# Two transformer blocks on one core: layer 0 as two streams with attention dealt among projections, expert weights in contiguous rows

## What is computed

```python
# first block, layer 0 (both streams) and layer 1 (x only, the context gives keys and values)
mx, mc = silu(c) @ ada_w[l] + ada_b[l], silu(c_ctx) @ ada_w[l] + ada_b[l]    # shift, scale, gate, twice
hx, hc = modulate(rmsnorm(x), mx), modulate(rmsnorm(ctx), mc)
yx, yc = mixer(hx, hc)      # layer 0: x attends to x (windowed or full) and to ctx; ctx attends to ctx only
x   = x   + gate_x * rmsnorm(yx);  x   = x   + gate_x2 * rmsnorm(swiglu(modulate(rmsnorm(x))))
ctx = ctx + gate_c * rmsnorm(yc);  ctx = ctx + gate_c2 * rmsnorm(swiglu(modulate(rmsnorm(ctx))))   # layer 0 only
# second block: h @ w_in, a gated recurrence (HGRN), a spatial gating unit, out projection, then
aff = softmax(h @ router_w);  gate, idx = top_k(aff.T, 32)                 # 16 experts choose 32 tokens each
hid = silu(xs @ w_gate) * (xs @ w_up)                                      # (32, 2048) per expert
x   = x + g_f * scatter_add((hid @ w_down) * gate)
```

## Time and profile before

| | us |
|---|---|
| median of 3 runs | 2781.61 (2778.0 to 2782.05) |
| the profiled execution | 2776.35 |
| its span | 2774.4 |
| PE busy in the span | 2235.6 (81%) |
| DVE, ACT busy | 576.9, 408.5 |
| HBM read | 610.49 MB, 220 GB/s over the span |

### The profile page before, as it was taken

The page is one execution under the profiler, slowest core; times in us unless marked ns, Lnnn a source line. Parts: engine busy times, 40 slices in busy tenths (PEclk is TensorE's granted clock), DMA queues, the critical chain, the costliest instruction groups (busy, mean ns, idle before and its releaser), DMA issues.

```text
span 2774.4 us, 25106 instructions
## 1 busy us (share of the span) xinstructions
PE 2235.6 (81%) x10537; PEld 1154.7 (42%) x10537; DVE 576.9 (21%) x1238; ACT 408.5 (15%) x814; POOL 6.2 (0%) x13
## 2 busy tenths in 40 slices
PE   6999988999999899899987789775555555565555
PEld 3444443444444446688834677641111111111111
DVE  3126823000000437200031582310000000000001
ACT  2014533000000325300032122110000000000000
POOL 0000000000000000000000000000000000000000
PEclk9999999999999999999999898987788778778876
DMA  9538841121222210243611231389999999999997
GB/s 367 219 160 307 314 138 61 61 81 42 63 78 68 91 61 31 92 151 103 201 61 61 70 112 70 129 342 418 417 416 417 418 418 418 418 416 416 417 418 300
DMA packets 198800, 613.17 MB, mean 221 GB/s; under 512 B 5360, under 2 KB 98800, under 8 KB 156448
## 3 DMA queue, kind: packets, MB, share of 16 engines
q1 hardware_dynamic: 197824, 608.28, 56.9%
q0 software_dynamic: 864, 3.28, 0.4%
HBM read 610.49 MB, written 1.05 MB: 220 GB/s over the span
## 4 chain that ended last, share of the span: by engine, by line
PE 48%; DMA 31%; DVE 5%; ACT 1%; issue 1%; DVEq 0%; ACTq 0%
PE ps L330 47%; DMA ring<-in_expert_w_up 12%; DMA ring<-in_expert_w_down 12%; DMA ring<-in_expert_w_gate 7%; PE ps L669 1%; DVE AR L635 1%; DVE X L636 1%; DVE AR L1254 0%; DVE AR L1242 0%; DVE AR L1243 0%; ACT H L581 0%; DVE AR L1135 0%; DVE AR L1231 0%; DVE AR L1232 0%; ACT RS L557 0%
## 5 line engine op out<-in xcount | busy, mean ns | idle before, releaser
L330 PE MATMUL ps<-ring,AR 128*32 128x512 f32 (+1 forms) x4096 | 523.2, 659 | 373.9 <-DMA ring<-in_expert_w_up 139.5
L330 PE MATMUL ps<-H,ring 128*128 128x512 f32 (+1 forms) x2416 | 800.5, 493 | 21.1 <-ACT H L581 13.1
L330 PEld LDWEIGHTS ps<-H,ring 128*128 128x128 f32 x2416 | 460.9, 192 | 353.2 <-issue 305.2
L330 PEld LDWEIGHTS ps<-ring,AR 128*32 128x32 f32 x4096 | 144.6, 134 | 735.8 <-issue 257.9
L330 PE MATMUL ps<-AR,ring 128*128 128x256 f32 (+1 forms) x1024 | 299.6, 456 | 3.0 <-DVE AR L793 1.5
L330 PEld LDWEIGHTS ps<-AR,ring 128*128 128x128 f32 x1024 | 196.1, 192 | 106.2 <-issue 84.4
L330 PE MATMUL ps<-AR 128*64 128x128 f32 (+5 forms) x1168 | 213.8, 340 | 29.6 <-DVE AR L1243 9.5
L330 PEld LDWEIGHTS ps<-AR 128*128 128x128 f32 (+2 forms) x1168 | 151.0, 186 | 108.9 <-issue 81.2
L1653 DVE TENSOR_TENSOR AR<-AR,ps 128x512 f32<-128x512 f32 x16 | 11.0, 688 | 590.9 <-PE ps L330 590.9
L793 DVE TENSOR_TENSOR AR<-AR,ps 128x512 f32<-128x512 f32 (+1 forms) x44 | 24.4, 555 | 424.7 <-PE ps L330 424.7
L1639 ACT ACTIVATE AR<-ps 128x512 f32<-128x512 f32 x16 | 9.6, 597 | 548.8 <-PE ps L330 548.8
(11 more groups left out here) (220 smaller groups left out, 1100.3 us busy)
## 6 DMA issues: line engine op xcount, KB each, us to landing
ring<-in_expert_w_gate SPq DMA_DIRECT2D x64, 2048.0 KB, 24.0
ring<-in_expert_w_up SPq DMA_DIRECT2D x64, 2048.0 KB, 23.4
ring<-in_expert_w_down SPq DMA_DIRECT2D x64, 2048.0 KB, 23.9
ring<-in_ada_w SPq DMA_DIRECT2D x36, 2048.0 KB, 8.6
ring<-in_ffn_w SPq DMA_DIRECT2D x44, 1024.0 KB, 7.1
ring<-in_ffn_w SPq DMA_DIRECT2D x16, 1408.0 KB, 7.1
ring<-in_w_in SPq DMA_DIRECT2D x11, 2048.0 KB, 7.9
ring<-in_ab_w_in SPq DMA_DIRECT2D x4, 2048.0 KB, 15.9
```

The costliest lines, as they stand in the source:

```text
L330: m = nc.tensor.matmul(out_, lhsT=lhsT, rhs=rhs, start=start, stop=stop)
```

## The change

1. **Two streams in layer 0.** x and the context become streams of 256 columns with their own semaphores. `Pre` and `Post` work on one half. The context is loaded first. The projections follow `AB_ORDER`: (stream, block) with 1 the context; two condition jobs stand between.
2. **Attention by stream.** 24 context units, then 24 x units, in each the differential ones first. The work beside a unit stands between its scores and its output product. Beside the context's units: x's last projection chunks (`AB_BESIDE`) and six condition jobs of layer 0 (`ADA_BESIDE`). Beside x's units: the twelve condition jobs of layer 1 in even units and the context's output projection in odd ones. Each stream's sub-norm goes beside its windowed units. For differential units scores are issued one unit less ahead.
3. **FFN0** runs the context three weight jobs ahead of x; norms of one stream go beside the blocks of the other. The context's latent projection follows x's last block.
4. **Layer 2's condition jobs** go beside layer 1's attention. The second context is loaded and normed beside FFN1's `w2` blocks.
5. **Norm sums**: DVE folds eight squares and PE sums one tile, where PE summed eight.
6. **Expert rows**: `runs` lays weights out as `(p k) n -> p k n`, one run of 16 KB per partition. The tokens and the hidden rows are read with strides 2 and 4 to match.
7. FFN gate and up products of two chunks share a bank.

The diff, cut to its core:

```diff
+HALF = (slice(0, TX), slice(TX, T2))
+LAG = 3
...
+        def runs(w, r0, r1):
+            k, n = (r1 - r0) // P, w.shape[-1]
+            return (lambda s: ring[:, s, 0:k * n].rearrange("p (k n) -> p k n", k=k),
+                    w[r0:r1, :].rearrange("(p k) n -> p k n", p=P))
...
-        ada_jobs(1)
-        ada_jobs(2)
-        for i in range(2):
-            job(("ab_out", i), rows(A["ab_w_out"][0], 0, D, i * 512, (i + 1) * 512))
+        ab_in_job(0)
+        ab_in_job(1)
+        ada_jobs(0, range(4, 6))
+        for i in range(2, 5):
+            ab_in_job(i)
+        ada_jobs(0, range(6, 12))
+        ada_jobs(1, range(4))
+        ab_out_jobs("ab_out_ctx", (0,))
+        ada_jobs(1, range(4, 8))
+        ab_out_jobs("ab_out_ctx", (1,))
+        ada_jobs(1, range(8, 12))
+        ab_out_jobs("ab_out", range(2))
         ffn_jobs(0)
...
         job("wkv_b", rows(A["mla_wkv_b"][0], 0, KVL, 0, 2048))
+        ada_jobs(2)
...
-                job(("gu", e, i), rows(w, (i % 4) * 256, (i % 4 + 1) * 256, 0, EF))
+                job(("gu", e, i), runs(w, (i % 4) * 256, (i % 4 + 1) * 256))
-                job(("dn", e, i), rows(A["expert_w_down_2"][0, e], i * 512, (i + 1) * 512, 0, D))
+                job(("dn", e, i), runs(A["expert_w_down_2"][0, e], i * 512, (i + 1) * 512))
...
         class Pre:
             def pe(self, pe):
+                pe.wait_ge(folded[self.half].sem, self.fold + KD - 1)
+                mm(ps[:, b, 0:TX], ones, self.ACC, True, True, b)
+            def dve_fold(self, c, k):
+                c.eng.wait_ge(squares_ready[self.half].sem, self.sq + k + 1)
+                first = H[:, 0, self.t] if k == 1 else self.ACC
+                c.mark(V.tensor_tensor(self.ACC, first, H[:, k, self.t], ALU.add), folded[self.half], self.fold + k)
...
+        def dve_norms(c, post, pre):
+            for k in range(KD):
+                post.dve_add(c, k)
+                if k >= 2:
+                    pre.dve_fold(c, k - 1)
+            pre.dve_fold(c, KD - 1)
+            pre.dve_scale(c)
...
         class Attention:
             def pe(self, pe):
                 for i, u in enumerate(self.units):
+                    while given < min(n, i + 4 - len(u.maps)):
+                        self.pe_scores(pe, given)
+                        given += 1
                     b = take(pe, ("t", u.key))
...
-                    if i + 3 < n:
-                        self.pe_scores(pe, i + 3)
+                    while given < min(n, i + 5 - len(u.maps)):
+                        self.pe_scores(pe, given)
+                        given += 1
+                    self.pe_beside(pe, i)
                     b = take(pe, ("o", u.key))
...
-                    if self.pe_beside:
-                        self.pe_beside(pe, i)
...
+        FFN0 = []
+        for i in range(NW + KD + LAG):
+            if i >= LAG:
+                FFN0.append((0, i - LAG))
+            if i < NW + KD:
+                FFN0.append((1, i))
...
+        AB_ORDER = [(1, 0), (1, 1), (1, 2), (0, 0), (1, 3), (0, 1), 4, 5, (1, 4), (0, 2)]
+        AB_BESIDE = {0: 10, 2: 11, 4: 12, 6: 13, 8: 14, 10: 15}
+        ADA_BESIDE = {13: 6, 14: 7, 16: 8, 17: 9, 18: 10, 19: 11}
...
+        def dve_item(c, s, n):
+            if s == 0:
+                for cq in turning(n):
+                    dve_rope(c, rope_base + ROPED.index(cq), QK[:, cq, 0:TX], ("rot", cq), TMP, ft("cos_ab"), ft("sin_ab"))
...
+        def pe_beside_x(pe, i):
+            pe_ada_beside(pe, 1, i)
+            if i % 2 and i < 16:
+                pe_out_chunk(pe, "yc", "ab_out_ctx", i // 2, lambda k: H[:, k, TX:T2])
+            pe_subln_beside(pe, 0, i)
+        def dve_beside_x(c, i):
+            dve_ada_beside(c, 1, i)
+            if i % 2 and i < 16:
+                post0a[1].dve_chunk(c, i // 2)
+            dve_subln_beside(c, 0, i)
...
-                        mm(ps[:, b, k * P:(k + 1) * P], HTOK[:, t, (4 * half + k) * P:(4 * half + k + 1) * P],
+                        mm(ps[:, b, k * P:(k + 1) * P], HTOK[:, t, (2 * half + k // 2) * 256 + k % 2:(2 * half + k // 2 + 1) * 256:2],
...
-                    m = nc.tensor.transpose(ps[:, b, i * P:(i + 1) * P], HS[:, i * P:(i + 1) * P], ident)
+                    m = nc.tensor.transpose(ps[:, b, i * P:(i + 1) * P], HS[:, i::4], ident)
```

More of the change, by code:

```diff
@@ L527, in pe_load @@
[L527 to L533, removed]
-                m.then_inc(bank_full[b], 1)
[L536 to L539, removed]
@@ L543, in act_squares, with pe_ada_beside, dve_ada_beside @@
-        def act_squares(c, base, chunks, src, sq, wait):
-            for k in range(chunks):
-                wait(c.eng, k)
-                c.mark(S.activation(sq(k), src(k), ACT.Square), squares_ready, base + k + 1)
+        def pe_ada_beside(pe, l, i):
+            if i in (8, 16, 24):
+                pe_ada_turn(pe, l, i // 8 - 1)
+            if i % 2 == 0 and i < 24:
+                pe_ada_job(pe, l, i // 2)
+        def dve_ada_beside(c, l, i):
+            if i in (7, 15, 23):
+                dve_ada_rows(c, l, i // 8)
+            if i in (9, 17, 25):
+                dve_ada_turned(c, l, i // 8 - 1)
@@ new lines, in pe_load, with dve_load @@
+        def pe_load(pe, name, stage, t0, loaded):
+            pe.wait_ge(loaded, 16)
+            for n in range(4):
+                b = take(pe, (name, n))
+                for a in range(2):
+                    for t in range(2):
+                        m = nc.tensor.transpose(ps[:, b, a * TX + t * P:a * TX + (t + 1) * P],
+                                                stage[:, t0 + t, (2 * n + a) * P:(2 * n + a + 1) * P], ident)
+                m.then_inc(bank_full[b], 1)
+        def dve_load(c, name, half):
+            for n in range(4):
+                b = full_of(c.eng, (name, n))
+                c.free(V.tensor_copy(X[:, 2 * n:2 * n + 2, HALF[half]], ps[:, b, :].rearrange("p (a t) -> p a t", a=2)),
+                       (name, n))
@@ L640, in build, with act_norms @@
+        def act_norms(c, post, pre):
+            post.act_rs(c)
+            pre.act(c, lambda e, k: e.wait_ge(x_ready[post.half].sem, post.x + k + 1))
+        def dve_norms(c, post, pre):
+            for k in range(KD):
+                post.dve_add(c, k)
[3 more added lines that the diff above has]
+            pre.dve_scale(c)
         PR = ar(12288, 2, 2, 512)
@@ new lines, in pe_w13 @@
+        def pe_w13(pe, l, i, s, pre=None):
+            w = weights(pe, ("w13", l, i)).rearrange("p (k n) -> p k n", k=KD)
+            for g, name in enumerate("gu"):
+                b = take(pe, (name, l, i, s))
+                for j in range(2):
+                    for k in range(KD):
+                        if pre is not None and g + j == 0:
+                            pre.ready(pe, k)
+                        mm(ps[:, b, j * TX:(j + 1) * TX], w[:, k, g * 256 + j * P:g * 256 + (j + 1) * P],
+                           H[:, k, HALF[s]], k == 0, k == KD - 1, b if j and k == KD - 1 else None)
+            if s == 0:
+                used()
@@ new lines, in pe_out_chunk, with pe_out @@
+        def pe_out_chunk(pe, name, label, n, Hf):
+            w = weights(pe, (label, n // 4)).rearrange("p (k n) -> p k n", k=KD)
+            b = take(pe, (name, n))
+            for k in range(KD):
+                mm(ps[:, b, 0:TX], w[:, k, n % 4 * P:(n % 4 + 1) * P], Hf(k), k == 0, k == KD - 1, b if k == KD - 1 else None)
+            if n % 4 == 3:
+                used()
+        def pe_out(pe, name, label, Hf, wait):
+            wait(pe)
+            for n in range(KD):
+                pe_out_chunk(pe, name, label, n, Hf)
```

821 lines of the change are left out of this document (483 added, 338 removed).

## The result

The changed kernel takes **2801.5 us** (median of four, 2800.0 to 2802.05) against 2781.8 for the kernel before (2778.0 to 2782.35): ratio **1.0073**, 95% interval 1.0055 to 1.009. It is slower by 20 us. The prediction said 2747 us, range 2706 to 2776, with 0.88 on faster: wrong in its sign and outside its range.

What follows compares the result with a forecast made beforehand. PE was taken as the bound up to 1811 us, then the load of expert weights. Savings of 12.4 us before the experts and 22 us in them, -34.4 us on the median 2781.61, gave 2747 us, range 2706 to 2776.

Steps and rivals of the forecast that it cites:

- projections, to the first probabilities: Layer 0's start: first matmul at 43.5 us, then 105.5 us of projections and 6.5 us to the first probabilities; 155.5 us.
- context attention and the second start: Layer 0: 24 context units with dealt work take 104 us, then a second pipeline start 6 us.
- x attention, with the last copy: Layer 0: 24 x units take 126 us, 49 differential and 77 windowed, and the last unit's copy 1.5; 127.5 us.
- output projection of x: Layer 0, after x's attention: 27.8 us of chunks and 4.8 us of waits; 32.6 us.
- FFN0 to layer 1's attention: FFN0 costs +4 us, less idle PE at the norm behind it saves 16.9 us; -12.9 us.
- layer 1's attention: Twelve condition jobs and three turns come on top, since PE is nearly full there; +26 us.
- from there to the experts: Behind layer 1's attention: norm folds +2.8 us, gap ahead of layer 2 -6.5, last norm -1.3; -5.0 us.
- expert stage: Expert weight stream: one 16 KB run per partition gives 427.5 GB/s where it had 417.4; -22 us.
- B: Expert stream: 16 KB runs are cut at 8 KB or run no faster, 9 instead of 22 us; 2760 us, chance 0.2.
- D: Expert stream: the long runs collide and it slows to 405 GB/s, +29 us; 2798 us, chance 0.06.
- The norms: Norm chain by folds 16.7 us for 13.9; gap ahead of layer 2 saves 6.5 us, the last norm 1.3.
- Rival C: Layer 0 attention: every unit takes bare cadence plus dealt work, 38 us more than counted; 2785 us, chance 0.06.

Runs made afterwards that it cites:

- filled_dealt: The kernel after with four idle matmuls on constant data ahead of the wait for probabilities in context units 1 to 11 only; 2794.4 us, ratio 1.0048.
- undealt_filled: undealt with four idle matmuls ahead of the wait for probabilities in context units 0 to 11; 2791.8 us, ratio 1.004.
- late_filled: The kernel after with VectorE's share of dealt pieces one unit later and six idle matmuls ahead of even context units 2 to 12; 2783.7 us.
- undealt: The kernel after with x's last six projection pieces done in one stretch ahead of the context attention; 2797.6 us, ratio 1.0053.

## Why the prediction was wrong, step by step

Forecast and measured, in us of span against the kernel before (misses add to 58.0, from -34.4 to +23.6):

| step of the prediction | forecast | measured | miss |
|---|---|---|---|
| projections, to the first probabilities | 155.5 | 157.9 | +2.4 |
| context attention and the second start | 104 + 6 | 134.4 | +24.4 |
| x attention, with the last copy | 127.5 | 142.5 | +15.0 |
| output projection of x | 32.6 | 36.2 | +3.6 |
| FFN0 to layer 1's attention | -12.9 | -4.1 | +8.8 |
| layer 1's attention | +26 | +22.6 | -3.4 |
| from there to the experts | -5.0 | +1.6 | +6.6 |
| expert stage | -22 | -21.4 | +0.6 |

- **Expert rows**: right in mechanism and size. 9 ns for each run and 151 ns for each 4 KB gave 427.5 GB/s; 428 was measured. Rivals B and D fell: the partitions' runs start 16 KB apart, and the middle of the stage has 428 GB/s for 417.
- **Context attention, the step that failed.** "a differential unit without company takes 3.7 us, and 7.7 us with a projection chunk": durations at full clock, put into an order that leaves TensorE idle. At full clock they nearly hold (filled_dealt: a pair 11.9 us, forecast 11.4; undealt_filled: 3.94 us bare, forecast 3.7). The kernel after had 0.77 there: units 0 to 7 took 53.3 us for 43, units 8 to 10 took 26.9 for 20.1. The wait was right, 2.46 us behind each rope (7.7 less TensorE's own 5.0 in my count); that waits also slow the work between them I left out, though the rows of before held it: 0.76 to 0.90 in five of the six short gaps, 0.95 and more beside them. The clock is not the whole of this miss of 17.1 us: the fillers took off 5.6 us alone and 10.0 us once the rope was late, and unit 10 with its value block takes 8.6 us (late_filled) or 10.4 (filled_dealt) near full clock, where I had 7.8.
- The thirteen last context units and the switch took 54.2 us for 47. The switch was 9.9 us behind a unit, and a unit with a condition job 3.40 us alone and 4.06 with the sum of a sub-norm, not 2.8: TensorE's own issue is 0.44 + 0.70 + 1.92 + 0.65 us there, overlapping a little, and I had added the job to VectorE's chain instead of taking the later of the two.
- **X attention.** The same slip: 4.5 to 5.3 us for windowed units with a condition job, which I priced at 4.1. Here it is not the clock, which was 1.00 in these units (345.8 to 396.9 us). The fold's wait was foreseen, and the late fold took 10 us off the stretch. The sum was low because most units of either kind with company cost 0.4 to 1.2 us more than counted, and a few up to 2.1 us more (the first unit 7.05 for 5.2, the last with an output chunk 8.94 for 6.8).
- **Output projection**: foreseen as a bank that ScalarE frees late (about 3 us). It was VectorE's copy behind the context's norms, 5.62 us (L513); with that gone ScalarE's wait showed, 3.60.
- **FFN0 to layer 1's attention**: 1.07, 2.41, 5.00 and 2.50 us of waits at 510, 925, 952 and 956 us, where the second pair was in the count. FFN0 came out 8.9 us longer for my 4.
- **Layer 2's jobs beside layer 1's attention**: +22.6 us for +26, right in kind and 3.4 high: TensorE was full there, and full it stayed (99.61 of 102.6 us busy) at clock 1.00.
- **The norms**: the chain behind layer 1's attention is 17.1 us for 16.7, right. The gap ahead of layer 2 fell by 6.0 us (17.3 for 23.3), where with its slow first chunk I had 8.3; what moved into FFN1 cost 3.3 us there for 1.9; and from layer 2 to the experts it is 0.9 us longer where I had 1.3 less.
- **Rival C** (the dealt order serializes fully, 2785 us) was the nearest in kind and had 0.06. It too lacked the clock. My check of the count against the old order (101 and 56 us for 103.5 and 56.5) proved less than I took from it: the old order kept TensorE busy (101.92 of 103.5 us at clock 0.95, 50.66 of 56.5 us at 1.00), so it could not show what idle time does.

The miss in layer 0 is 45.4 us. Against the kernel after, 12.5 us went with the later rope and fold, 5.4 us more with the fillers, 12.9 us with the joined pipeline and the earlier copy: 30.7 us together, by the medians. These are not all parts of the miss: the late rope also avoids a wait that the forecast had counted, and the joined pipeline a part of the second start, for which it had 6 us. The slow clock is what the prediction lacked in kind; by the fillers it accounts for some 6 to 10 us of the context's miss, an estimate. The larger part of the number is the sizes of single units and of the two starts. The rest (under-priced units of either stream, FFN0's waits) was not removed by any run, and what norms by folds in place of sums on TensorE cost by themselves was not tried.

## What to carry to other kernels

Here unit prices came from stretches in which TensorE is full, and were prices at full clock (FFN0 of before: 455.56 of 456.5 us busy, clock 1.00). Before such prices are put into an order with waits, look at the granted clock of the stretches that have waits of that kind (here 0.76 to 0.90 in five of the six short gaps), and price the pieces at both levels (here 3.47 and up to 6.05 us for a key piece). Dealt work whose finishing step (here VectorE's rope) stood ahead of the next thing that the path needs did not hide: TensorE waited 2.46 us behind the rope. In a queue that runs in order, place the finishing step one unit later, which took 12.5 us off here. Even then dealing the projections was worth too little to be told here, so try the plain order too. And test independent parts of a change apart: here one part was worth 23 to 24 us and the other cost 44.

## What the runs showed that I had not expected

- Extra matmul instructions whose result nobody reads made the kernel faster (2791.8 us for 2797.6): 88 more in the window of twelve units (undealt_filled against undealt), granted clock 0.50 to 1.00, 49.4 to 43.5 us for the same VectorE work.
- TensorE can be busy for 37.2 of 49.4 us and be granted 0.50 of full speed throughout (undealt, 185.1 to 234.5 us). At that clock it is busy longer (2.38 us for a bare unit's eight score instructions, 1.37 at 1.00 in undealt_filled), which hides in the busy column what the clock column shows.
- The two causes help each other: the late rope alone took 5.3 us off the eleven units with dealt work, the fillers alone 5.6, both together 15.3.
- And one that I had expected: one run of 16 KB for each partition streams at 428 GB/s (417 before), as the shorter runs let one extrapolate, though the partitions' runs start 16 KB apart.
